# Weaving the two token blocks of the activations that are only stationary

## Chip, core and metric

One core of a Trainium2 chip runs the kernel. The metric is the device time of one execution in microseconds, the median of several runs. TensorE is called PE here, VectorE DVE, ScalarE ACT, GpSimd POOL, and SyncE SP.

## What is computed

256 tokens of width 1024 go through two blocks of two layers each; everything is float32. Cut to what matters here:

```
# block 1, two layers
proj = rms_norm(x, g_mix[l]) @ w_in[l]                 # 1024 x 10052
... four branches y_a, y_b, y_c, y_d, each ending in a @ w_o*[l] (512 x 1024)
merged = sum over branches of sigmoid(gate + b_gate) * y
x = x + merged @ w_merge[l]                             # 1024 x 1024
h2 = rms_norm(x, g_ffn[l])
gt = causal_dwconv(h2 @ w_ffn_gate[l], ffn_conv_w[l])   # 1024 x 2816
x = x + (silu(gt) * (h2 @ w_ffn_up[l])) @ w_ffn_down[l] # 2816 x 1024

# block 2, two layers
proj = rmsnorm(x, norm_w[l]) @ w_in[l]
y = concatenate([y_mla, y_gdn, y_moba])                 # 256 x 1024
x = x + y @ w_out[l]                                    # 1024 x 1024
```

## The kernel before

Weights stream from HBM into a ring of three slots of one megabyte (issued by SP, L2703). Each slot is cut into two parts, counted by `j`. For every part ACT writes a rounded high half, `whi` (L1173, `split_hi`, type fp32r), and DVE the remainder, `wlo` (L1755, `split_lo`); four parts are in flight, and both engines run four parts ahead of PE. The activations have the same two halves: `hhi` and `hlo` (8 channel chunks of 128 partitions x 256 tokens), `F[q] = (fhi, flo)` (4 chunks each) and, in block 2, `W0` and `W3` (2 chunks each, one tensor `fin`). A product is three passes in fp32r: high x high, low activation x high weight, high activation x low weight.

There are two ways to multiply a part:

- `chans` (from L484): the weights are the stationary operand (128 x 128) and the activation moves, 256 tokens. Output: channels by tokens. L499 holds the passes with `whi`, L508 that with `wlo`. A part has 24 matmuls of 256 columns.
- `toks` (from L512): 128 tokens of the activation are the stationary operand and 512 (in two places 324 and 416) weight columns move. Output: tokens by channels. L521 has the passes with `whi`, L529 that with `wlo`. A part of 512 columns has 12 matmuls: two token blocks `u`, two channel chunks `k`, three passes. `last_pair` (from L533, lines L544 and L551) does the last two parts of an accumulation, token block by token block.

`toks` and `last_pair` read the stationary operand as `s_[:, k0 + k, cols(u)]`: 128 tokens that lie side by side, 4 bytes apart; `cols(u)` is `slice(u * 128, u * 128 + 128)`.

Where `toks` and `last_pair` are used: some input projections of block 1 (`idx`, `aq`, `ak`, `av`, `sv`) and `m0` of block 2, all on the normed `hhi`/`hlo`, which `chans` also reads as the moving operand; the merge (merged activations, again written into `hhi`/`hlo` after the last use of the normed ones); FFN-down (`F`, the gated activations); and w_out of block 2 (`W0` and `W3` for chunks 0 and 3, `hhi`/`hlo` for 1 and 2, in the order 0, 3, 1, 2 of `OUT_ORDER`).

Who writes these: ACT copies the f32 values (`mer1`, `fy`, `yT`) into the high tensor (L1440 and L1449 for the merge, L1480 for the FFN, L1630 for block 2), and DVE subtracts that from the f32 values into the low one (L2175, L2255, L2545). All work on 2 chunks x 256 tokens. PE waits for the low one before the first part that needs it. The program of every engine is written out in order; side tasks (convolution, attention, delta rule) are interleaved with the parts at fixed places (`MIX_AT`, `TWO_AT`). Other matmuls go through two helpers, L469 (`group`) and L474 (`turn`, transposes), in plain f32.

## Time and profile before

| | |
|---|---|
| median of 3 runs | 1377.38 us (1377.34 to 1378.05) |
| span of the profiled execution | 1369.2 us |
| PE busy | 1345.0 us (98%), 10828 matmuls |
| DVE busy | 1040.0 us (76%) |
| ACT busy | 750.9 us (55%) |
| HBM read | 221.01 MB, mean 162 GB/s |

The span goes from the first to the last instruction of one profiled execution; of that execution the profile gives no other time. Engine rows give busy time, share of the span and instruction counts. A matmul is pipelined: its recorded duration overlaps the next one's, so what it costs a stream is the distance from its start to the next start. PEld is the load of the stationary operand, which goes on under the matmul before. In a group, the text `out<-moving,stationary` is followed by the rows and columns of the array that are in use and the number of partitions and elements of the moving operand; for PEld these are the stationary operand's. A row of busy times by stretch holds start:end, its length, then the busy time of PE, PEld, DVE, ACT and POOL with their counts, the granted clock, the share of the DMA engines and GB/s.

### The profile page before, as it was taken

To read this page: it belongs to the slowest core of one execution; us is meant where nothing else is said; L and a number is where in the kernel's file an instruction comes from. 1 tells how busy PE (TensorE), PEld (TensorE's weight loads), DVE (VectorE), ACT (ScalarE), POOL (GpSimd) and SP (SyncE) were. 2 spreads that over 40 slices of the span, in tenths; PEclk is the share of its full clock that TensorE was granted. 3 is DMA by queue.
4 is the path that set the end of the run, shared out by engine and by line. 5 is a ranking of instruction groups with operands and counts; after the bars stand their busy time and mean duration, and the time that the engine had idled before them with its cause. 6 is when DMAs were issued, how large, how long until landed. Compare 5 with 4: busy or idle time off the path is not lost. (4 is left out here: it accounts for less than half of the span.)

```text
span 1369.2 us, 26498 instructions
## 1 busy us (share of the span) xinstructions
PE 1345.0 (98%) x10828; PEld 1265.4 (92%) x10828; DVE 1040.0 (76%) x1781; ACT 750.9 (55%) x1157; POOL 46.3 (3%) x48
## 2 busy tenths in 40 slices
PE   8999999999999999999999999999999999999998
PEld 8899999998999989899999999999989899888996
DVE  6999898677766666999897767766778746777565
ACT  6544656556444455544557545544558546576363
POOL 0000000000000000000000000000000110001100
PEclk9999999999999999999999999999999999999999
DMA  8565444564665465645364555555553324353231
GB/s 289 177 207 178 131 154 160 180 215 155 197 202 185 139 230 163 215 155 185 97 204 159 187 187 172 198 185 191 178 186 124 120 64 137 100 174 109 78 102 69
DMA packets 108992, 223.77 MB, mean 163 GB/s; under 512 B 6180, under 2 KB 17700, under 8 KB 108872
## 3 DMA queue, kind: packets, MB, share of 16 engines
q1 hardware_dynamic: 106736, 219.12, 48.2%
q10 hardware_dynamic: 2136, 2.96, 0.7%
q8 instruction: 86, 1.41, 0.4%
q14 instruction: 34, 0.28, 0.1%
HBM read 221.01 MB, written 1.06 MB: 162 GB/s over the span
## 5 line engine op out<-in xcount | busy, mean ns | idle before, releaser
L1755 DVE TENSOR_TENSOR wlo<-ring,whi 128x1024 fp32r<-128x1024 f32 (+3 forms) x430 | 498.1, 1180 | 182.7 <-ACT whi L1173 152.7
L1173 ACT ACTIVATE whi<-ring 128x1024 fp32r<-128x1024 f32 (+3 forms) x430 | 433.2, 1026 | 361.8 <-PE bank L499 228.7
L499 PE MATMUL bank<-hhi,whi 128*128 128x256 f32 x2016 | 278.8, 280 | 6.0 <-ACT sgb L1431 3.9
L508 PE MATMUL bank<-hhi,wlo 128*128 128x256 f32 x2016 | 280.3, 281 | 0.0
L499 PE MATMUL bank<-hlo,whi 128*128 128x256 f32 x2016 | 275.3, 278 | 0.0
L499 PEld LDWEIGHTS bank<-hhi,whi 128*128 128x128 f32 x2016 | 253.1, 189 | 9.5 <-ACT sgb L1431 4.3
L508 PEld LDWEIGHTS bank<-hhi,wlo 128*128 128x128 f32 x2016 | 252.6, 189 | 3.7 <-issue 2.6
L499 PEld LDWEIGHTS bank<-hlo,whi 128*128 128x128 f32 x2016 | 251.6, 189 | 0.0
L469 PE MATMUL bank<-w 64*64 64x64 f32 (+5 forms) x1376 | 101.7, 249 | 1.5 <-DMA w<-in_flip 0.9
L1935 DVE SCALAR_TENSOR_TENSOR w<-w,par 128x256 f32<-128x256 f32 x240 | 98.0, 478 | 0.0
L521 PE MATMUL bank<-whi,hhi 128*128 128x512 f32 (+2 forms) x256 | 96.6, 379 | 0.0
L521 PE MATMUL bank<-whi,hlo 128*128 128x512 f32 (+2 forms) x256 | 96.1, 377 | 0.0
L469 PEld LDWEIGHTS bank<-w 64*64 64x64 f32 (+3 forms) x1376 | 84.1, 150 | 10.7 <-issue 2.6
L2615 POOL TENSOR_TENSOR st<-st,mhalf 128x1 f32<-128x1 f32 (+2 forms) x34 | 33.3, 979 | 1224.9 <-DVE st L1776 558.0
L529 PE MATMUL bank<-wlo,hhi 128*128 128x512 f32 (+2 forms) x256 | 65.2, 377 | 0.0
L521 PE MATMUL bank<-whi,flo 128*128 128x512 f32 x160 | 62.6, 392 | 0.0
L521 PE MATMUL bank<-whi,fhi 128*128 128x512 f32 x160 | 62.5, 391 | 0.0
L521 PEld LDWEIGHTS bank<-whi,hhi 128*128 128x128 f32 x256 | 48.1, 188 | 8.9 <-issue 0.9
L521 PEld LDWEIGHTS bank<-whi,hlo 128*128 128x128 f32 x256 | 48.1, 188 | 7.6
L529 PEld LDWEIGHTS bank<-wlo,hhi 128*128 128x128 f32 x256 | 47.0, 188 | 8.0
L529 PE MATMUL bank<-wlo,fhi 128*128 128x512 f32 x160 | 43.2, 392 | 0.0
L2238 DVE SCALAR_TENSOR_TENSOR w<-w,par 128x256 f32<-128x256 f32 x88 | 36.7, 478 | 0.0
(309 smaller groups left out, 1535.5 us busy)
## 6 DMA issues: line engine op xcount, KB each, us to landing
ring<-in_w_in SPq DMA_DIRECT2D x100, 1024.0 KB, 5.1
ring<-in_w_ffn_down SPq DMA_DIRECT2D x22, 1024.0 KB, 5.1
ring<-in_w_ffn_gate SPq DMA_DIRECT2D x20, 1024.0 KB, 5.1
ring<-in_w_ffn_up SPq DMA_DIRECT2D x20, 1024.0 KB, 5.1
ring<-in_w_merge SPq DMA_DIRECT2D x8, 1024.0 KB, 5.1
ring<-in_w_out SPq DMA_DIRECT2D x8, 1024.0 KB, 5.0
ring<-in_w_oc SPq DMA_DIRECT2D x4, 1024.0 KB, 5.3
ring<-in_w_od SPq DMA_DIRECT2D x4, 1024.0 KB, 5.2
```

Of the source, the lines that this page charges most:

```text
L469: done = e.matmul(o, l_, r_, start=start and i == 0, stop=stop and i == len(pairs) - 1)
L499: done = e.matmul(o, wh[:, k, cols(u)], s_[:, k0 + k, :], stop=False, skip_group_check=True, start=opens and k == 0 and s_ is sh and u % 2 ...
L508: done = e.matmul(o, wl[:, k, cols(u)], sh[:, k0 + k, :], start=False, stop=closes, skip_group_check=True)
L521: done = e.matmul(held[u][:, 0:n], s_[:, k0 + k, cols(u)], wh[:, k, 0:n], stop=False, start=opens and k == 0 and s_ is sh, skip_group_chec ...
L529: done = e.matmul(held[u][:, 0:n], sh[:, k0 + k, cols(u)], wl[:, k, 0:n], start=False, stop=closes, skip_group_check=True)
L1173: e.activation(part_of(whi, j), part_raw(j), ACT.Copy).then_inc(*up("hi.a"))
L1755: e.tensor_tensor(part_of(wlo, j), part_raw(j), part_of(whi, j), ALU.subtract).then_inc(*up("lo.v"))
L1935: e.scalar_tensor_tensor(out=cacc[:, c], in0=glup[:, c, j:j + S], scalar=wv, in1=cacc[:, c], op0=ALU.mult, op1=ALU.add).then_inc(*up(name))
L2238: e.scalar_tensor_tensor(out=y, in0=g, scalar=wv, in1=y, op0=ALU.mult, op1=ALU.add).then_inc(*up("ffn.v"))
L2615: e.tensor_tensor(dst, src, half(n), ALU.pow).then_inc(*up(name))
```

## The change

Two views are added. `woven_toks` reads a tensor's 256 token places as 128 pairs: token `t * 128 + i` lies at place `2 * i + t`, so the tokens of one block are 8 bytes apart, with the other block's between them. `plain_toks` gives the same four dimensions on a contiguous tensor. The writers of the merged, gated and block-2 activations (ACT's copy and DVE's subtraction) write through `woven_toks`, and the merge, FFN-down and w_out read their stationary operands through it. The input projections read through `plain_toks`, which gives the same addresses as before. No instruction is added or removed, and no wait or queue changes.

```diff
--- before.py
+++ after.py
@@ -248,6 +248,12 @@
 
         def cols(h):
             return slice(h * P, h * P + P)
+
+        def woven_toks(ap):
+            return ap.rearrange("p c (i t) -> p c t i", t=2)
+
+        def plain_toks(ap):
+            return ap.rearrange("p c (t i) -> p c t i", t=2)
 
 
         A1, B1, vAf = part1(0, 1024), part1(1024, 1024), part1(2048, 1024)
@@ -509,16 +515,16 @@
                                         skip_group_check=True)
                 done.then_inc(*up("second.p"))
 
-            def toks(j, held, n, src, k0, opens, closes, mid=None):
+            def toks(j, held, n, src, k0, opens, closes, mid=None, weave=False):
 
                 wh, wl = part_of(whi, j), part_of(wlo, j)
-                sh, sl = src
+                sh, sl = (woven_toks(s_) if weave else plain_toks(s_) for s_ in src)
                 kn = wh.shape[1]
                 e.wait_ge(SEM["hi.a"], j + 1)
                 for u in range(2):
                     for k in range(kn):
                         for s_ in (sh, sl):
-                            done = e.matmul(held[u][:, 0:n], s_[:, k0 + k, cols(u)], wh[:, k, 0:n], stop=False,
+                            done = e.matmul(held[u][:, 0:n], s_[:, k0 + k, u], wh[:, k, 0:n], stop=False,
                                             start=opens and k == 0 and s_ is sh, skip_group_check=True)
                 done.then_inc(*up("first.p"))
                 if mid:
@@ -526,14 +532,14 @@
                 low_ready(j)
                 for u in range(2):
                     for k in range(kn):
-                        done = e.matmul(held[u][:, 0:n], sh[:, k0 + k, cols(u)], wl[:, k, 0:n], start=False, stop=closes,
+                        done = e.matmul(held[u][:, 0:n], sh[:, k0 + k, u], wl[:, k, 0:n], start=False, stop=closes,
                                         skip_group_check=True)
                 done.then_inc(*up("second.p"))
 
             def last_pair(j, acc, src, k0, tag, l):
 
 
-                sh, sl = src
+                sh, sl = (woven_toks(s_) for s_ in src)
                 for tb in range(2):
                     for nh in range(2):
                         wh, wl = part_of(whi, j + nh), part_of(wlo, j + nh)
@@ -541,14 +547,14 @@
                             e.wait_ge(SEM["hi.a"], j + nh + 1)
                         for k in range(2):
                             for s_ in (sh, sl):
-                                done = e.matmul(acc[nh][tb][:, :], s_[:, k0 + k, cols(tb)], wh[:, k, :], start=False,
+                                done = e.matmul(acc[nh][tb][:, :], s_[:, k0 + k, tb], wh[:, k, :], start=False,
                                                 stop=False, skip_group_check=True)
                         if tb == 0:
                             low_ready(j + nh)
                         else:
                             done.then_inc(*up("first.p"))
                         for k in range(2):
-                            done = e.matmul(acc[nh][tb][:, :], sh[:, k0 + k, cols(tb)], wl[:, k, :], start=False, stop=True,
+                            done = e.matmul(acc[nh][tb][:, :], sh[:, k0 + k, tb], wl[:, k, :], start=False, stop=True,
                                             skip_group_check=True)
                         if tb == 0:
                             done.then_inc(*up("norm.p"))
@@ -766,7 +772,7 @@
                 for c in range(3):
                     e.wait_ge(*at("mlo", l, c))
                     for nh in range(2):
-                        toks(j, [acc[nh], acc[2 + nh]], 512, hh, 2 * c, c == 0, False)
+                        toks(j, [acc[nh], acc[2 + nh]], 512, hh, 2 * c, c == 0, False, weave=True)
                         j += 1
                 e.wait_ge(*at("mlo", l, 3))
                 last_pair(j, [[acc[nh], acc[2 + nh]] for nh in range(2)], hh, 6, "mix", l)
@@ -779,7 +785,7 @@
                     for k in range(0, n, 2):
                         e.wait_ge(*at("f", l, i6, k // 2))
                         for nh in range(2):
-                            toks(j, [acc[nh], acc[2 + nh]], 512, F[i6 % 2], k, i6 == 0 and k == 0, False)
+                            toks(j, [acc[nh], acc[2 + nh]], 512, F[i6 % 2], k, i6 == 0 and k == 0, False, weave=True)
                             j += 1
                             put("second.p", "down", l, i6, nh)
                     return j
@@ -1124,7 +1130,7 @@
                     for nh in range(2):
                         if n == 0:
                             acc[nh] = [ps.take(e, "m", "wout", l, 2 * tb + nh) for tb in range(2)]
-                        toks(j, acc[nh], 512, src, k0, n == 0, False, between(j))
+                        toks(j, acc[nh], 512, src, k0, n == 0, False, between(j), weave=True)
                         behind(j)
                         j += 1
 
@@ -1437,7 +1443,8 @@
                                 if q == 0:
                                     e.wait_ge(*at(name, "gate", l, hf))
                                 e.wait_ge(*at("merged", l, 3, q))
-                                e.activation(hhi[:, 2 * q:2 * q + 2], mer1[:, 2 * q:2 * q + 2], ACT.Copy).then_inc(*up("mix.a"))
+                                e.activation(woven_toks(hhi[:, 2 * q:2 * q + 2]), plain_toks(mer1[:, 2 * q:2 * q + 2]),
+                                             ACT.Copy).then_inc(*up("mix.a"))
                                 put("mix.a", "mhi", l, q)
                         for i in range(2):
                             side.run(MIX_AT.get(2 * (j - mix0(l)), ()))
@@ -1446,7 +1453,8 @@
                             j += 1
                 for q in range(2, 4):
                     e.wait_ge(*at("merged", l, 3, q))
-                    e.activation(hhi[:, 2 * q:2 * q + 2], mer1[:, 2 * q:2 * q + 2], ACT.Copy).then_inc(*up("mix.a"))
+                    e.activation(woven_toks(hhi[:, 2 * q:2 * q + 2]), plain_toks(mer1[:, 2 * q:2 * q + 2]),
+                                 ACT.Copy).then_inc(*up("mix.a"))
                     put("mix.a", "mhi", l, q)
                 for i in range(6):
                     split_to(j + 4)
@@ -1477,7 +1485,8 @@
                         e.wait_ge(*at("fy", l, i6, i))
                         if i6 > 1:
                             e.wait_ge(*at("down", l, i6 - 2, 1))
-                        e.activation(F[i6 % 2][0][:, 2 * i:2 * i + 2], fy[:, 2 * i:2 * i + 2], ACT.Copy).then_inc(*up("ffn.a"))
+                        e.activation(woven_toks(F[i6 % 2][0][:, 2 * i:2 * i + 2]), plain_toks(fy[:, 2 * i:2 * i + 2]),
+                                     ACT.Copy).then_inc(*up("ffn.a"))
                         put("ffn.a", "f", "hi", l, i6, i)
                     for i in range(4 if i6 else 0):
                         split_to(j + 4)
@@ -1627,7 +1636,7 @@
                         e.wait_ge(*at("mla" if c == 0 else "moba", "gated", l))
                         e.wait_ge(*at("mla", "lg", l, 1, 1))
                         dst = (W0 if c == 0 else W3)[0]
-                    e.activation(dst, yT[:, 2 * c:2 * c + 2], ACT.Copy).then_inc(*up("outs.a"))
+                    e.activation(woven_toks(dst), plain_toks(yT[:, 2 * c:2 * c + 2]), ACT.Copy).then_inc(*up("outs.a"))
                     put("outs.a", "fin", "hi", l, c)
 
 
@@ -2172,8 +2181,8 @@
 
                 def low_v(q):
                     e.wait_ge(*at("mhi", l, q))
-                    e.tensor_tensor(hlo[:, 2 * q:2 * q + 2], mer1[:, 2 * q:2 * q + 2], hhi[:, 2 * q:2 * q + 2],
-                                    ALU.subtract).then_inc(*up("mix.v"))
+                    e.tensor_tensor(woven_toks(hlo[:, 2 * q:2 * q + 2]), plain_toks(mer1[:, 2 * q:2 * q + 2]),
+                                    woven_toks(hhi[:, 2 * q:2 * q + 2]), ALU.subtract).then_inc(*up("mix.v"))
                     put("mix.v", "mlo", l, q)
 
                 for n_b, (key, bi, name, _) in enumerate(BRANCHES):
@@ -2252,7 +2261,8 @@
                         leave("ffn.v", "up", l, i6, i)
                         put("ffn.v", "fy", l, i6, i)
                         e.wait_ge(*at("f", "hi", l, i6, i))
-                        e.tensor_tensor(F[i6 % 2][1][:, 2 * i:2 * i + 2], y2, F[i6 % 2][0][:, 2 * i:2 * i + 2],
+                        e.tensor_tensor(woven_toks(F[i6 % 2][1][:, 2 * i:2 * i + 2]), plain_toks(y2),
+                                        woven_toks(F[i6 % 2][0][:, 2 * i:2 * i + 2]),
                                         ALU.subtract).then_inc(*up("ffn.v"))
                         put("ffn.v", "f", l, i6, i)
                     for i in range(4 if i6 else 0):
@@ -2542,7 +2552,7 @@
                         e.tensor_tensor(y2, y2, g, ALU.mult).then_inc(*up("outs.v"))
                         put("outs.v", tag, "gated", l)
                     e.wait_ge(*at("fin", "hi", l, c))
-                    e.tensor_tensor(lo, y2, hi, ALU.subtract).then_inc(*up("outs.v"))
+                    e.tensor_tensor(woven_toks(lo), plain_toks(y2), woven_toks(hi), ALU.subtract).then_inc(*up("outs.v"))
                     put("outs.v", "fin", l, c)
 
 
```

## Rows read from the trace of the kernel before

**Rows 1.** The page: span, busy times, granted clock and GB/s in 40 slices.

```profile
span 1369.2 us, 26498 instructions
...
PE 1345.0 (98%) x10828; PEld 1265.4 (92%) x10828; DVE 1040.0 (76%) x1781; ACT 750.9 (55%) x1157; POOL 46.3 (3%) x48
...
PEclk9999999999999999999999999999999999999999
...
GB/s 289 177 207 178 131 154 160 180 215 155 197 202 185 139 230 163 215 155 185 97 204 159 187 187 172 198 185 191 178 186 124 120 64 137 100 174 109 78 102 69
```

**Rows 2.** The waits of PE: total, times, longest; the largest.

```profile
PE bank L499 <- ACT sgb L1431: 3.9, 2, 2.0
```

**Rows 3.** Groups by form of PE: count | busy us, mean ns | idle before.

```profile
L521 PE MATMUL bank<-whi,hhi 128*128 128x512 f32 x192 | 75.5, 393 | 0.0
...
L521 PE MATMUL bank<-whi,fhi 128*128 128x512 f32 x160 | 62.5, 391 | 0.0
...
L521 PE MATMUL bank<-whi,fin 128*128 128x512 f32 x64 | 16.1, 394 | 0.0
...
L544 PE MATMUL bank<-whi,hhi 128*128 128x512 f32 x32 | 12.5, 391 | 0.0
...
L544 PE MATMUL bank<-whi,fhi 128*128 128x512 f32 x16 | 6.3, 391 | 0.0
```

**Rows 4.** Timeline of PE, merge and FFN-down: start us, us, instruction.

```profile
301.91 0.39 PE L521 MATMUL bank<-whi,hhi 128*128 128x512 f32 x1
...
304.66 0.39 PE L521 MATMUL bank<-whi,hhi 128*128 128x512 f32 x1
...
318.39 0.39 PE L544 MATMUL bank<-whi,hhi 128*128 128x512 f32 x1
...
371.96 0.39 PE L521 MATMUL bank<-whi,fhi 128*128 128x512 f32 x1
372.19 0.39 PE L521 MATMUL bank<-whi,flo 128*128 128x512 f32 x1
```

**Rows 5.** Timeline: plain f32 matmuls of 256 columns; loads under one-column matmuls.

```profile
226.52 1.89 PE L469 MATMUL bank<-xn 128*128 128x256 f32 x8
...
1334.84 1.87 PEld L469 LDWEIGHTS bank<-onesb,w 128*128 128x128 f32 x16
```

**Rows 6.** Timeline of PE: 324 columns, 512 in another rhythm, 256.

```profile
36.77 0.31 PE L521 MATMUL bank<-whi,hhi 128*128 128x324 f32 x1
...
38.55 0.31 PE L521 MATMUL bank<-whi,hhi 128*128 128x324 f32 x1
...
98.34 0.40 PE L521 MATMUL bank<-whi,hhi 128*128 128x512 f32 x1
...
101.15 0.40 PE L521 MATMUL bank<-whi,hhi 128*128 128x512 f32 x1
...
298.29 1.07 PE L508 MATMUL bank<-fhi,wlo 128*128 128x256 f32 x8
```

**Rows 7.** Writers (by form; by line: count, min/median/max, first and last start); a stretch's busy times.

```profile
L1480 ACT ACTIVATE fhi<-w 128x512 fp32r<-128x512 f32 x22 | 13.9, 632 | 41.0 <-DVE w L2251 41.0
...
L2255 DVE TENSOR_TENSOR flo<-w,fhi x22: 691/693/694, 354.4 to 997.1; 128x512 fp32r<-128x512 f32 x22
...
L2175 DVE TENSOR_TENSOR hlo<-w,hhi x4: 684/692/694, 298.8 to 308.3; 128x512 fp32r<-128x512 f32 x4
...
372.00:383.00 11.00, 11.00 (x51) 9.03 (x50) 8.53 (x9) 6.15 (x8) 0.00 (x0) 1.00 0.50 165
```

**Rows 8.** Timeline of w_out in the last layer, all engines.

```profile
1348.86 1.99 PE L521 MATMUL bank<-whi,fin 128*128 128x512 f32 x8
...
1350.42 1.29 DVE L2545 TENSOR_TENSOR hlo<-w,hhi 128x512 fp32r<-128x512 f32 x2
...
1351.38 0.19 PEld L521 LDWEIGHTS bank<-whi,hhi 128*128 128x128 f32 x1
```

## Prediction

> **What bounds the kernel now.** I read the page first, its shares and its 40 slices. TensorE (PE) is busy 98% of a span of 1369.2 us, in nearly every slice, at a granted clock of 9 tenths or more in all of them, the level of 2.4 GHz; VectorE (DVE) is busy 76% and ScalarE (ACT) 55% [rows 1]. Then the waits of PE: the largest adds up to 3.9 us, and none stands on the lines that the change touches, L521, L529, L544 and L551 (the row kept is the largest) [rows 2]. So what PE does between the starts of two matmuls sets the time, and a nanosecond there is worth its count. The median of the runs is 1377.38 us, 8.2 us above the profiled span (what lies around the span and between runs); I make the sum against the span and carry it over to the median unchanged.
>
> The groups by form give the counts. The woven matmuls are those with an activation as the stationary operand (128x128) and 512 weight columns moving: L521 fhi 160 + flo 160, L529 fhi 160, L544 fhi 16 + flo 16, L551 fhi 16, that is 528 for FFN-down; L521 fin 64 (high and low) and half as many on L529, that is 96; L544 hhi 32 + hlo 32 and L551 hhi 32, that is 96 (of each name one row stands; its low twin and its second pass have the same count) [rows 3]. Of the three groups of 192 on hhi and hlo at L521 and L529, a third each is woven: by the loops, merge has 2 layers x 3 chunks x 2 halves of N x 4 matmuls = 48 and w_out's third chunk 2 x 2 x 4 = 16, so 64 a group, 192 together [rows 3]. In all 528 + 96 + 96 + 192 = 912. The other 3 x 128 = 384 with 512 columns belong to the block-1 input projections, where hhi is also a moving operand elsewhere; they keep the contiguous layout.
>
> The number to look at is not a matmul's recorded duration (391 ns, pipelined) but the distance between starts. In the merge the parts of 12 matmuls start at 301.91, 304.66 and so on, and the 72nd matmul after the first starts at 318.39: 16.48 us / 72 = 228.9 ns [rows 4]. FFN-down starts its second matmul 0.23 us after the first, and the eight of w_out take 1.99 us, (1.99 - 0.39) / 7 = 229 ns [rows 4, 8]. There is no idle time in those rows. I use 229.0 ns. At 2.4 GHz 512 columns are 213.3 ns, so 15.7 ns of each are not columns.
>
> **What the 15.7 ns may be.** Each matmul has a load of 128 columns under it. The load is not the bound: with one moving column 16 loads take 1.87 us, (1.87 - 0.19) / 15 = 112 ns apiece [rows 5], half of 229. Plain f32 matmuls with 256 columns take 1.89 us for eight, (1.89 - 0.379) / 7 = 215.9 ns: they spend two array cycles a column, so the same 213.3 ns of array time and the same load of 128 columns, with 2.6 ns on top [rows 5]. What differs is that their moving operand is read half as fast. So 13.1 ns appear only where the moving operand is read at 4 bytes per array cycle. Two more observations. The excess is mostly not proportional to the columns: with 324 columns a part of twelve takes 38.55 - 36.77 = 1.78 us, 148.3 ns each, of which 135.0 are columns, 13.3 ns of excess against 15.7 [rows 6]. And the same instructions on the same tiles come in another rhythm elsewhere: 101.15 - 98.34 = 2.81 us for twelve, 234 ns each [rows 6]. An excess that changes while shapes, tiles and clock stay is an interference that depends on how two streams fall against each other, and the two streams of PE are the load and the moving operand. With 256 columns (32 matmuls from 298.29 to 301.91, 113.1 ns) the load's 112 ns binds and says little [rows 6].
>
> **The change, part by part.** (1) The step of the load. Before, the load walks 128 x 4 = 512 bytes in 112 ns, 4.6 bytes/ns, while the moving operand walks 2048 bytes in 213.3 ns, 9.6 bytes/ns: one overtakes the other, and they can meet again and again. Woven, the load walks 1024 bytes in 112 ns, 9.1 bytes/ns, nearly abreast of the moving operand. After a first meeting both keep their distance. No row shows a load with this step, so the price is bounded: it may take away all 13.1 ns, down to the nearest row without interference, 215.9 ns (the bare columns would be 213.3, 15.7 ns less), or nothing, or it may add as much again, 13.1 ns, if what costs is the address range that the load touches, which doubles. I take the full removal, because the f32 row has the same array time and load and sits at 215.9, and the rates match: 912 x 13.1 ns = 11.9 us less. The bounds are -14.3 us and +11.9 us.
>
> The page "TensorE: Matmul & The Clock Gate" of the Trainium skill (section on what happens when you issue a matmul) says that the load and the streaming operand have independent SBUF read ports and that the load takes nothing from a running matmul. The rows above have 13.1 ns that this rule doesn't explain; by the rule the sum would be 0 and the time stay. The page "SBUF — State Buffer" (Specifications) states cachelines of 16 bytes that want at least two hits each: a step of 8 bytes just has its two, so no slower load, but 64 lines instead of 32. If each line opened costs the moving operand something, that rule speaks against the change.
>
> (2) The writers. 22 ACT copies of 632 ns for FFN, and by the loops 8 for the merge and 8 for w_out, write with the step now, 38 in all, and as many DVE subtractions of about 692 ns [rows 7]. Whether the step slows them no row shows. Between 0 and twice as long, that is 0 to 24 us of ACT and 0 to 26 us of DVE over engines idle 45% and 24% of the span [rows 1]; below nothing is excluded, since the element count is the same. I take 0. The cover: FFN's first low part starts at 354.4 and is first used at 371.96, 17 us later; the merge's first starts at 298.8 for a matmul at 301.91, and its last at 308.3 for those at 318.39 [rows 4, 7]. Doubling them reaches none of these. Queued behind them on ACT and DVE are the weight splits of the next parts. In a stretch of FFN-down DVE is busy 8.53 of 11.00 us and ACT 6.15 [rows 7]; with PE through in 10.4 us DVE stands at 82%, and with each of its subtractions twice as long (two in a chunk of 33 us) hardly higher.
>
> (3) What is late next. In w_out chunk 1 waits for its low part: the pair of subtractions starts at 1350.42, of the two, 1.29 us together, the first ends near 1351.1, and the load that needs it is at 1351.38, 0.27 us of slack [rows 8]. The four parts before it (48 matmuls) shrink by 0.6 us. The subtraction is queued behind a weight split on DVE, and that behind ACT's, which partly follow PE; so the new wait is 0 to 0.36 us per layer. I take 0.1 us per layer, 0.2 together. If the writers were twice as long, 0.7 us per layer would come on top at this one place. DMA: in the same stretch its engines are busy half the time at 165 GB/s, and 6% more is far under the 289 GB/s of the first slice [rows 1, 7].
>
> Sum: 1377.4 - 11.9 + 0.2 = 1365.7 us.
>
> **Rivals.**
> A. Half of it. The meeting remains in part, or the load itself takes longer because each 16 of its elements now spread over twice the bytes: at twice 112 ns the load would bind at 224 ns, 5 ns less than now, 912 x 5 = 4.6 us; half the interference gone is 6.0 us. Time about 1371 to 1373. For it: two streams of 9.1 and 9.6 bytes/ns still drift by some 60 bytes in a load.
> B. Nothing. The 15.7 ns belong to a moving operand read at full rate, whatever the load does; the step changes nothing and the writers are hidden. 1377.4 us, 0.2 us up at most. The independent ports of the skill's page on TensorE would make it this case. For it: 324 and 512 columns can be read as a line with 0.429 ns a column and 9.2 ns fixed, and nothing in it must be a collision. Against: the second rhythm of 234 ns.
> C. Slower. Each load touches twice the range, and each new piece of it stops the moving operand: 13.1 ns become 26.2, the start distance 242, 912 x 13.1 = 11.9 us more, 1389.3 us. It shows as slower once the distance is over 229.0 + 2.75 us / 912 = 232 ns. For it: 234 ns exist already in this trace, so worse meetings are possible; and abreast can also mean always in the same place. Against: 2.4 GHz columns stalled once lag by that much for good, and a stalled stream leaves the place.
>
> **How the numbers follow.** Full removal 0.52 (0.03 of it down to the bare columns, 1363.1), A 0.16, B 0.17, C 0.15. The predicted time is that of the full removal, 1365.7 us. The range holds full removal, A and B: from 1362.5 (bare columns, less the spread of runs) to 1378.0 (B with the small wait and the spread); C's 0.15 is left out. 0.2% of 1377 is 2.75 us, about what a measurement of this kernel can tell from no change; full removal and A are beyond it: faster 0.68, same 0.17, slower 0.15.
>
> **What would show it.** Right: the starts on L521, L529, L544 and L551 with fhi, flo and fin 216 ns apart, a merge part every 2.59 us, while the 384 contiguous ones of the input projections stay at 229 and 234 and the 256-column ones at 113. The two-sided price: a distance near 224 points to a slower load, one above 232 to rival C. Writers: the rows of L1480 and L2255 at 632 and 692 ns. Wrong would be the whole argument if the contiguous ones moved with them, or if PE's waits gained a row on hhi, hlo, fhi or flo of over 1 us.

## Result and the profile after

The changed kernel takes 1383.47 us (median, 1382.14 to 1384.55); the kernel before, on the same chip, 1377.36 us (1373.62 to 1378.05). The ratio is 1.0048, with a 95% interval of 1.0031 to 1.0066: slower by 0.5%, where 11.7 us less was forecast, and outside the range of 1362.5 to 1378.0.

The page of after, with the lines that answer [rows 1]:

```profile
span 1382.8 us, 26498 instructions
...
PE 1359.0 (98%) x10828; PEld 1281.9 (93%) x10828; DVE 1040.4 (75%) x1781; ACT 752.0 (54%) x1157; POOL 46.2 (3%) x48
...
PEclk9999999999999999999999999999999999999999
```

The instruction count is the same, PE is again busy 98%, at 9 tenths or more in every slice. The span is 13.6 us longer, and PE is busy 14.0 us more, at the same number of matmuls. The waits of PE show nothing new; the largest is the one of [rows 2], unchanged:

```profile
PE bank L505 <- ACT sgb L1437: 3.9, 2, 2.0
```

So matmuls became slower, and the timeline of PE in the first FFN-down of after says which (start us, us, instruction; line L527 is L521 of before, L505 is L499, L514 is L508; matmuls of flo and of L535 between are left out, x8 stands for eight in a row):

```profile
303.75 0.40 PE L527 MATMUL bank<-whi,hhi 128*128 128x512 f32 x1
...
306.56 0.39 PE L527 MATMUL bank<-whi,hhi 128*128 128x512 f32 x1
...
374.21 0.40 PE L527 MATMUL bank<-whi,fhi 128*128 128x512 f32 x1
...
377.02 0.39 PE L527 MATMUL bank<-whi,fhi 128*128 128x512 f32 x1
...
385.42 1.10 PE L505 MATMUL bank<-hhi,whi 128*128 128x256 f32 x8
386.36 1.10 PE L505 MATMUL bank<-hlo,whi 128*128 128x256 f32 x8
387.30 1.10 PE L514 MATMUL bank<-hhi,wlo 128*128 128x256 f32 x8
...
391.07 1.11 PE L505 MATMUL bank<-hhi,whi 128*128 128x256 f32 x8
```

A woven part of twelve takes 2.81 us, in the merge as in FFN-down, where it took 2.75 in [rows 4]. Four parts, 48 matmuls, take 385.42 - 374.21 = 11.21 us, 233.5 ns each against 229.0. And there is a second thing, which the change does not touch in the code at all: the matmuls of 256 columns behind it, the gate weights of the FFN, take 391.07 - 385.42 = 5.65 us for 48, 117.7 ns each. The same place in the timeline of before:

```profile
382.95 1.09 PE L499 MATMUL bank<-hhi,whi 128*128 128x256 f32 x8
383.88 1.07 PE L499 MATMUL bank<-hlo,whi 128*128 128x256 f32 x8
384.79 1.07 PE L508 MATMUL bank<-hhi,wlo 128*128 128x256 f32 x8
```

There eight of them take 384.79 - 383.88 = 0.91 us, 113.4 ns each (the next ones as well; only the first eight take 0.93). I call 113.4 ns the fast rhythm of the narrow matmuls (256 columns) and 117.7 the slow one. Both occur in both kernels, with PE never idle in them: a stretch keeps its rhythm over hundreds of matmuls, and it changes only where other matmuls or a wait come between. Behind FFN-down it is fast in all eight stretches of before (in each of two layers three of 192 matmuls and one of 96) and slow in all eight of after.

The bill for the 13.6 us between the two spans:

- 912 woven matmuls x 4.4 ns = 4.0 us.
- 1344 narrow matmuls behind FFN-down x 4.3 ns = 5.8 us. As a test of both terms together: a layer's FFN-down with what stands behind it holds 264 woven and 672 narrow ones, 1.16 + 2.89 = 4.05 us; counted off matmul by matmul the difference grows by 4.02 us over it in either layer.
- 1.6 us near 1225 us, where the granted clock of after falls to half for some 3 us and that of before does not:

```profile
1225.00:1226.00 1.00, 1.00 (x9) 1.00 (x8) 1.00 (x4) 0.92 (x4) 0.00 (x0) 0.64 0.16 59
1226.00:1227.00 1.00, 1.00 (x6) 1.00 (x6) 1.00 (x3) 0.99 (x2) 0.00 (x0) 0.50 0.01 4
```

  (Busy times of PE, PEld, DVE, ACT and POOL by stretch, then the granted clock, 1.00 for 2.4 GHz and 0.50 for 1.2.) A wait for DVE stands just before it in both kernels, 1.22 us in after and 1.24 in before. Of the ten traces of the whole kernel shown or named below, the clock falls here in five (after, e3_writers, e5_settled, e7_before_settled and e11_rest_only), with and without woven reads, and in five not (before, e4, e2, e6, e10); after and e10 are the same kernel. So it is chance and not the weave. Two more such falls, near 170 and 670 us, stand in both traces and so not in the bill.
- 0.9 us in the first 12 us (a wait for the first input: the first narrow matmul starts at 12.94 us instead of 12.00) and 0.8 us in the first 192 narrow matmuls, which are in the slow rhythm here and in the fast one in before; both lie ahead of the first woven instruction.

That is 13.1 of 13.6 us; the rest is small differences of both signs. The first two entries, 9.8 us, go with the weave, the other 3.3 us don't. The medians are only 6.1 us apart: the timed runs of before took some 6 us more than its traced one, and on what is not known, since none of them was traced. In the other comparisons below the kernel before has medians of 1370.95, 1371.11 and 1375.51 us.

What of the prediction's other rows answers: the contiguous matmuls did not move (the 144 of the input projections from 43.88 us on start 229.0 ns apart in both traces). The writers, by form (busy us, mean ns, idle before), to be held against [rows 7], and the load of the woven operand:

```profile
L527 PEld LDWEIGHTS bank<-whi,fhi 128*128 128x128 f32 x160 | 31.3, 196 | 6.0
...
L2264 DVE TENSOR_TENSOR flo<-w,fhi 128x512 fp32r<-128x512 f32 x22 | 15.3, 696 | 16.2 <-ACT fhi L1488 16.2
...
L1488 ACT ACTIVATE fhi<-w 128x512 fp32r<-128x512 f32 x22 | 14.7, 668 | 40.7 <-DVE w L2260 40.7
```

ACT's copy is 36 ns longer (632 in before), DVE's subtraction 3 (693). The load's record says 196 ns; before it said 188:

```profile
L521 PEld LDWEIGHTS bank<-whi,fhi 128*128 128x128 f32 x160 | 30.0, 188 | 6.2
```

In w_out the third term's wait did not come, since the woven parts did not shrink: chunk 1's low part is written from 1363.76 us on (a pair of 1.29 us, the first done near 1364.45), and its load starts at 1364.78, with 0.33 us to spare.

### The profile page after: what moved, and what is told of

Read it like the earlier page. It is cut to its first block and busy times, and to the rows that moved or that the text cites. A ratio compares the mean times of both kernels' runs of the same rounds, so it can differ in the third digit from the quotient of the medians.

```text
span 1382.8 us, 26498 instructions
## 1 busy us (share of the span) xinstructions
PE 1359.0 (98%) x10828; PEld 1281.9 (93%) x10828; DVE 1040.4 (75%) x1781; ACT 752.0 (54%) x1157; POOL 46.2 (3%) x48
## 5 line engine op out<-in xcount | busy, mean ns | idle before, releaser
L505 PE MATMUL bank<-hhi,whi 128*128 128x256 f32 x2016 | 280.9, 281 | 6.2 <-ACT sgb L1437 3.9
L514 PE MATMUL bank<-hhi,wlo 128*128 128x256 f32 x2016 | 283.3, 282 | 0.0
L505 PE MATMUL bank<-hlo,whi 128*128 128x256 f32 x2016 | 278.1, 280 | 0.0
L505 PEld LDWEIGHTS bank<-hhi,whi 128*128 128x128 f32 x2016 | 255.0, 189 | 9.6 <-ACT sgb L1437 4.3
L514 PEld LDWEIGHTS bank<-hhi,wlo 128*128 128x128 f32 x2016 | 255.4, 190 | 3.7 <-issue 2.6
L505 PEld LDWEIGHTS bank<-hlo,whi 128*128 128x128 f32 x2016 | 254.0, 189 | 0.0
L1944 DVE SCALAR_TENSOR_TENSOR w<-w,par 128x256 f32<-128x256 f32 x240 | 98.1, 478 | 0.0
L527 PE MATMUL bank<-whi,hhi 128*128 128x512 f32 (+2 forms) x256 | 97.0, 380 | 0.0
L527 PE MATMUL bank<-whi,hlo 128*128 128x512 f32 (+2 forms) x256 | 96.4, 378 | 0.0
L535 PE MATMUL bank<-wlo,hhi 128*128 128x512 f32 (+2 forms) x256 | 65.5, 378 | 0.0
L527 PE MATMUL bank<-whi,fhi 128*128 128x512 f32 x160 | 63.4, 396 | 0.0
L527 PE MATMUL bank<-whi,flo 128*128 128x512 f32 x160 | 63.2, 395 | 0.0
L527 PEld LDWEIGHTS bank<-whi,hhi 128*128 128x128 f32 x256 | 48.6, 190 | 8.8 <-issue 0.9
L527 PEld LDWEIGHTS bank<-whi,hlo 128*128 128x128 f32 x256 | 48.5, 190 | 7.3
L535 PEld LDWEIGHTS bank<-wlo,hhi 128*128 128x128 f32 x256 | 47.4, 190 | 7.8
L535 PE MATMUL bank<-wlo,fhi 128*128 128x512 f32 x160 | 43.8, 395 | 0.0
L527 PEld LDWEIGHTS bank<-whi,fhi 128*128 128x128 f32 x160 | 31.3, 196 | 6.0
```

The source lines that it names most:

```text
L505: done = e.matmul(o, wh[:, k, cols(u)], s_[:, k0 + k, :], stop=False, skip_group_check=True, start=opens and k == 0 and s_ is sh and u % 2 ...
L514: done = e.matmul(o, wl[:, k, cols(u)], sh[:, k0 + k, :], start=False, stop=closes, skip_group_check=True)
L527: done = e.matmul(held[u][:, 0:n], s_[:, k0 + k, u], wh[:, k, 0:n], stop=False, start=opens and k == 0 and s_ is sh, skip_group_check=True)
L535: done = e.matmul(held[u][:, 0:n], sh[:, k0 + k, u], wl[:, k, 0:n], start=False, stop=closes, skip_group_check=True)
L1944: e.scalar_tensor_tensor(out=cacc[:, c], in0=glup[:, c, j:j + S], scalar=wv, in1=cacc[:, c], op0=ALU.mult, op1=ALU.add).then_inc(*up(name))
```

## Experiments

Theory 1, after this reading: the load of an 8-byte step is itself longer, this costs the woven matmuls 4.4 ns each, and the rhythm in which PE leaves them is handed on to the narrow ones behind (this last part did not hold as a rule, see under e3_writers). Its rivals: the writers do it; what follows is chance of one run; the narrow ones are slow for a reason of their own.

**e1_micro: the step by itself.** A small kernel without the computation, in which only the step of the stationary operand differs:

```
for s in (1, 2, 3, 4, 8):            # step in elements of 4 bytes
    stationary = g[s][:, c].rearrange("p (i t) -> p t i", t=s)[:, u]
    # 12, 24 ... matmuls of 512 columns, between narrow ones of 256
```

> A kernel of its own that leaves out the whole computation and only streams matmuls: 24-matmul blocks of 256 columns with weights as the stationary operand, three times twelve matmuls of 512 columns whose stationary operand has a step of 4, 8, 12, 16 or 32 bytes, then 256 columns again; each stretch after a short pause; then loads under 64 moving columns, and plain f32 matmuls of 256 columns, by step. Theory 1 (the step disturbs the stream): 229 ns between starts at 4 bytes, 233 to 234 at 8 bytes as in the changed kernel, more at 16 and 32, since fewer elements share a neighbourhood; the load under 64 columns stays at 112 ns at 4 and 8 bytes. Theory 2 (only the rhythm that a stretch happens to start with): 229 or 234 at every step, mixed between the two passes over the steps. Theory 3 (inherited rhythm): the 256-column matmuls after a stretch of 4 bytes settle at 113.4 ns, those after 8 bytes at 117.7, whatever the ones before had.

Timeline of PE, first the step of 4 bytes, then of 8 (x8 of high and low, L221 between them left out):

```profile
256.66 1.98 PE L217 MATMUL bank<-whi,g 128*128 128x512 f32 x8
...
267.54 1.98 PE L217 MATMUL bank<-whi,g 128*128 128x512 f32 x8
...
273.57 2.03 PE L217 MATMUL bank<-whi,g 128*128 128x512 f32 x8
...
284.77 2.03 PE L217 MATMUL bank<-whi,g 128*128 128x512 f32 x8
```

48 matmuls take 10.88 us at 4 bytes, 226.7 ns each, and 11.20 us at 8 bytes, 233.3 ns. Over all passes it was 227 at 4 bytes, 233.0 at 8, 235 at 12 and at 16, 244.6 at 32. So the step costs some 6 ns here with no ACT, DVE or DMA at work: it is a matter of PE and its reads alone. But the narrow matmuls ran at about 120 ns after every step; the handing on (Theory 3) did not show in this kernel. The loads under 64 columns missed too: at a granted clock of 1.00 they took 112 ns at 4 bytes, but 117 to 118 at 8, where 112 was expected. Plain f32 matmuls of 256 columns had 215.8 ns at both steps.

**e2_readers and e3_writers: halves of the change.** In the first only the reads of the stationary operands are woven, and the writers store contiguously:

```diff
-e.activation(woven_toks(F[i6 % 2][0][:, 2 * i:2 * i + 2]), plain_toks(fy[:, 2 * i:2 * i + 2]), ACT.Copy)
+e.activation(plain_toks(F[i6 % 2][0][:, 2 * i:2 * i + 2]), plain_toks(fy[:, 2 * i:2 * i + 2]), ACT.Copy)
```

and so for the other writers; in the second it is the reverse:

```diff
-                sh, sl = (woven_toks(s_) if weave else plain_toks(s_) for s_ in src)
+                sh, sl = (plain_toks(s_) for s_ in src)
```

> Only the readers weave: merge, FFN-down and w_out load their stationary operand with 8 bytes from tensors written contiguously, so the tokens come out in another order; everything else as before. Theory 1 (the loads do it): all of the loss, ratio 1.004 to 1.005 to the kernel before, 233.3 ns on the 912 matmuls and 117.7 ns on the 256-column ones behind FFN-down. Rival (the writers do it): ratio 1.000, 229 ns.

> Only the writers weave, the readers load 128 neighbouring places, which now hold tokens of both blocks (order changed, amount of work the same). Theory 1 (the loads do it): ratio 1.000, 229 ns, 632 ns a copy on ScalarE and 692 ns a subtraction on VectorE as before. Rival (the step of the writes costs, or delays a split behind it): ratio 1.004, and longer copies or PE waits.

Reads alone: 1382.89 us, ratio 1.0084 (1.0067 to 1.0101). Writers alone: 1372.1 us, ratio 1.0008 (0.9999 to 1.0018). The reads carry the loss; the writers' 36 and 3 ns are covered, as the prediction said. Two numbers expected were missed: the ratio of the reads, 1.004 to 1.005, and the copy of e3_writers, 632 ns, which took 667 (632 in e2_readers). The load's record is 195 ns in e2_readers and 188 in e3_writers. The first FFN-down in the timeline of e3_writers, where the reads are contiguous:

```profile
374.96 0.40 PE L527 MATMUL bank<-whi,fhi 128*128 128x512 f32 x1
...
386.16 1.09 PE L505 MATMUL bank<-hhi,whi 128*128 128x256 f32 x8
387.09 1.07 PE L505 MATMUL bank<-hlo,whi 128*128 128x256 f32 x8
387.99 1.07 PE L514 MATMUL bank<-hhi,wlo 128*128 128x256 f32 x8
```

This one stretch is a surprise: contiguous, and yet 11.20 us for 48, 233.3 ns. In this run the 384 narrow matmuls ahead of it were in the slow rhythm; the seven other FFN-down stretches, entered from fast narrow ones, have 228.9. So a contiguous stretch can be slow too, when it is entered in the slow rhythm. (The first FFN-down of e11_rest_only is a second case. The 24 contiguous ones of [rows 6], from 98.34 us on, bear it out as well: they have 228.8 ns in the three cases of twenty in which the narrow ones ahead are fast, and 233.4 to 233.5 in the seventeen in which those are slow.) But the stretch of e3_writers leaves the fast rhythm behind: 0.90 to 0.91 us for eight. In e2_readers the same happens once in each layer (entered slow, left fast); the other six of its eight narrow stretches are slow. The handing on is therefore a strong tendency of the woven loads and not a law.

Nor is it the stretch's own distance that is handed on. In the timeline of before, the 144 contiguous matmuls of the input projections, 229.0 ns apart, leave slow narrow ones behind them without any pause:

```profile
75.07 1.10 PE L499 MATMUL bank<-hhi,whi 128*128 128x256 f32 x8
76.02 1.11 PE L499 MATMUL bank<-hlo,whi 128*128 128x256 f32 x8
```

0.95 us for eight. It is so in both layers of all nine traces in which nothing is inserted there, 18 of 18. A contiguous stretch can thus leave either rhythm, and what decides between this place and FFN-down no run shows. What the runs do show is that at FFN-down the weave turns what stands behind from fast to slow.

**e4_before_again: how much a run of before differs from another.** The kernel before, unchanged.

> The kernel before, once more. Its first profile has a span of 1369.2 us, while three of four timed runs are at 1377 us; the changed kernel's profile lies within 2 us of its timed runs. Theory (the 256-column streams take one of two rhythms, 113.4 or 117.7 ns, partly by chance of where they start): this profile has about 6 us more than the first, all of it in 256-column streams at 117.7 that were at 113.4. Rival (the time lies outside the matmul streams): the streams show the same rhythms as the first profile.

1369.6 us, span 1367.8. This missed: I had looked for the several microseconds between the profiled run and the median of before, and this run is again a short one, its span 1.4 us below the first. Its rhythms aren't quite those of the first trace: the 144 narrow matmuls from 81.5 us on (`sq`, `sk`) are fast here and slow there (-0.7 us with what is behind them). Larger is a difference that is no rhythm: in the first trace the granted clock falls to half for 3.4 us near 168 us, and here it does not (-1.6 us); a wait of 0.94 us at 193.58 us, which the first does not have, and slow narrow matmuls give the 1.5 us back.

```profile
168.00:169.00 1.00, 1.00 (x7) 1.00 (x6) 1.00 (x2) 0.14 (x1) 0.00 (x0) 0.50 0.00 0
```

(The first trace.) Rhythms, falls of the clock and the first wait thus all vary from run to run. The kernel before takes 1369 to 1378 us in its runs; which of the three makes the longer ones long is not shown, as none of them was traced. Behind FFN-down all eight are fast again.

**e5_settled: undo the handing on, keep the weave.** Two plain f32 matmuls of one column between each woven FFN-down and the narrow ones:

```diff
+            def settle(o, n=2):
+                for _ in range(n):
+                    e.matmul(o[:, 0:1], onesb[:, :], onesb[:, 0:1], start=True, stop=True)
@@ chans
+                if opens and j in [ffn0(l_) + 20 + 12 * q_ for l_ in range(L) for q_ in range(4)]:
+                    settle(held[0])
```

> The changed kernel with two one-column f32 matmuls before the first matmul of each gate group that follows an FFN-down (4 places a layer, 16 matmuls of about 112 ns, 1.8 us in all). In five traces a stretch of 256-column matmuls behind one-column matmuls ran at 113.4 ns every time (10 of 10), behind the woven FFN-down at 117.7 in 13 of 17. Theory (the woven stretch hands its slower rhythm on, and that is more than half of the loss): these stretches go to 113.4, 1344 x 4.3 ns = 5.8 us less, with the cost 4 us less than the changed kernel, about 1379 us; the woven matmuls stay at 233.3. Rival (the slower 256-column matmuls have their own cause): 117.7 stays, the time is 2 us over the changed kernel's.

```profile
371.59 0.40 PE L534 MATMUL bank<-whi,fhi 128*128 128x512 f32 x1
...
382.79 0.50 PE L493 MATMUL bank<-onesb 128*128 128x1 f32 x4
383.15 1.16 PE L512 MATMUL bank<-hhi,whi 128*128 128x256 f32 x8
384.15 1.07 PE L512 MATMUL bank<-hlo,whi 128*128 128x256 f32 x8
385.06 1.07 PE L521 MATMUL bank<-hhi,wlo 128*128 128x256 f32 x8
```

(Each f32 matmul of one column has two records, so x4 is the two.) The woven stretch takes 382.79 - 371.59 = 11.20 us for 48, as in after, while the narrow ones behind are fast again, 385.06 - 384.15 = 0.91 us for eight, in all eight places. Both claims hold: the 4.4 ns belong to the woven loads, and the 4.3 ns of the narrow ones are no cost of the narrow ones' own. The insertion itself costs 0.36 us until the next narrow start and 0.09 more in the first eight, 0.45 us each, 3.6 in all, so a gain of 5.8 - 3.6 = 2.2 us over the changed kernel should be left, where 4 were expected. The median is 1379.2 us, ratio 1.0063 (1.0046 to 1.008) against a before of 1370.95 in that comparison. The changed kernel did not run in it, so the gain itself isn't measured. It is no way back to the time of before.

**e6_down_only and e11_rest_only: the change in two pieces.** Only FFN-down and its writers woven (528 matmuls), and only the merge and w_out (384):

```diff
 # e6_down_only
-                sh, sl = (woven_toks(s_) for s_ in src)
+                sh, sl = ((woven_toks if tag == "ffn" else plain_toks)(s_) for s_ in src)
 # e11_rest_only
-                sh, sl = (woven_toks(s_) for s_ in src)
+                sh, sl = ((plain_toks if tag == "ffn" else woven_toks)(s_) for s_ in src)
```

with `weave=True` and the writers of the other piece taken back as well.

> Only FFN-down is woven; merge and w_out are written and read as before. Theory (own cost 4.4 ns on 528 matmuls, 2.3 us, plus the inherited rhythm on up to 1344 narrow matmuls, 5.8 us): about 8 us of the change's loss of 10 to 12 stays, ratio 1.005 to 1.007. Rival (only the matmuls' own cost, in proportion to their number 528 of 912): ratio 1.002 to 1.003.

> Only merge and w_out are woven (384 of the 912 matmuls), FFN-down as before. Behind merge and w_out come norms with pauses, so there is no narrow stretch to inherit. Theory (own cost plus inheritance): 384 x 4.4 ns = 1.7 us, ratio 1.001 to 1.002, and the stretches behind FFN-down at 113.4. Rival (the loss has another source, common to all woven parts): in proportion 384 / 912 of the whole, 1.0035.

FFN-down alone: 1379.96 us, ratio 1.0067 (1.0052 to 1.0082); that is 9.2 us (7.1 to 11.2) where the two terms give 528 x 4.4 ns + 5.8 us = 8.1 us. The rest alone: 1376.71 us, ratio 1.0006 (0.9995 to 1.0018), 0.8 us (-0.7 to 2.5) where 384 x 4.4 ns give 1.7. Both hold within their intervals. Two timelines, of e6_down_only behind its second woven stretch:

```profile
416.85 1.10 PE L505 MATMUL bank<-hhi,whi 128*128 128x256 f32 x8
417.79 1.11 PE L505 MATMUL bank<-hlo,whi 128*128 128x256 f32 x8
418.74 1.10 PE L514 MATMUL bank<-hhi,wlo 128*128 128x256 f32 x8
```

and of e11_rest_only, the same stretch, contiguous, and what is behind it:

```profile
407.25 0.39 PE L527 MATMUL bank<-whi,fhi 128*128 128x512 f32 x1
...
418.23 1.10 PE L505 MATMUL bank<-hhi,whi 128*128 128x256 f32 x8
419.17 1.07 PE L505 MATMUL bank<-hlo,whi 128*128 128x256 f32 x8
420.07 1.07 PE L514 MATMUL bank<-hhi,wlo 128*128 128x256 f32 x8
```

0.94 to 0.95 us for eight against 0.90, and 10.98 us for the 48 of 512 columns, 228.8 ns.

**e7_before_settled: the same insertion in the kernel before**, ahead of its slow narrow stretches:

```diff
@@ chans (before)
+                if opens and j in [j_ for l_ in range(L) for j_ in (mix0(l_), mix0(l_) + 24, mix0(l_) + 28, mix0(l_) + 44, ffn0(l_))]:
+                    settle(held[0])
```

> The kernel before with the same two one-column matmuls before five groups of a layer whose narrow matmuls often run at 117.7 ns (glu_b, sq, sk, gb and the FFN's first gate): 20 extra matmuls, 2.2 us. If they settle the rhythm, up to 5 x 96 x 2 narrow matmuls gain 4.3 ns, 4.1 us, and the time falls by about 2 us with less spread; if not, it rises by 2 us.

1377.66 us, ratio 1.0055 (1.004 to 1.007): missed. Behind seven of the ten insertions the narrow matmuls are fast, behind three they are slow. Two of the three even stand between 48 narrow matmuls at 113.4 ns and 96 at 117.7 ns; this is the timeline of the first:

```profile
88.13 0.50 PE L487 MATMUL bank<-onesb 128*128 128x1 f32 x4
...
89.52 1.10 PE L506 MATMUL bank<-hlo,whi 128*128 128x256 f32 x8
90.46 1.11 PE L515 MATMUL bank<-hhi,wlo 128*128 128x256 f32 x8
```

(0.94 us for eight behind it, 0.91 ahead.) So the insertion does not set the fast rhythm everywhere, as it did in the eight places of e5_settled. In each layer 48, 48 of 144 and 160 of 240 slow narrow matmuls became fast, 2.2 us in both layers, and each of the ten insertions costs 0.45 us as above, 4.5 us. That is 2.3 us more. By the last FFN-down of block 1 this trace is 3.1 us behind the one of before (995.72 against 992.66 us), of which 1.0 us lies in the first wait, ahead of the first narrow matmul, and 2.0 are left for the insertions. Of the 6.5 us between the two spans the rest lies in block 2, which has no insertion: 0.8 us up to 1190 us, 1.0 in waits behind that, and the fall of the clock for 1.6. The rhythm of the narrow matmuls can be bent by hand, but not at a profit in this way, and the price of the insertion was set too low: 2.2 us for the twenty extra matmuls, where they cost 4.5.

**e8_micro2: an attempt to bring the fast rhythm about outside the kernel**, with the tensors at the places that they have in the kernel, and narrow stretches behind 512-column ones at both steps, one-column ones and plain f32 ones:

```
[narrow 24] [512 columns x24, step 4 or 8 bytes] [narrow 48]
[narrow 24] [f32, 1, 128, 256 or 512 columns]     [narrow 48]
```

> A kernel of its own without the computation: the tensors lie as in the real kernel; after a pause one part of 24 narrow matmuls, then something else, then two parts narrow; the something is 2 or 4 parts of 512 columns at 4 or at 8 bytes, one, two or four f32 matmuls of one column, f32 ones of 128, 256 or 512 columns; three times each. Theory (the rhythm is a relation in time between load and moving operand that the last matmuls leave behind): 512 columns at 4 bytes run at 229 and leave 113.4 behind; at 8 bytes they run at 233.3 and leave 117.7 more often than not; the one-column ones leave 113.4. Rival (chance): both rhythms behind each of them, in no relation.

```profile
32.10 0.39 PE L216 MATMUL bank<-whi,hhi 128*128 128x512 f32 x1
...
37.69 1.10 PE L229 MATMUL bank<-hhi,whi 128*128 128x256 f32 x8
...
46.65 0.39 PE L216 MATMUL bank<-whi,hhi 128*128 128x512 f32 x1
...
52.25 1.11 PE L229 MATMUL bank<-hhi,whi 128*128 128x256 f32 x8
```

At 4 bytes 5.59 us for 24, 232.9 ns, at 8 bytes 5.60, 233.3. Narrow ones settled at 117 to 119 ns throughout, and nothing put ahead of them brought 113.4. So this kernel is in the slow rhythm all the time, and in it both steps cost the same. That agrees with the contiguous stretch of 233.3 in e3_writers and says nothing on how the fast rhythm comes about. Inconclusive for its purpose.

**e9_micro3: is the excess over the columns a matter of the load at all?** With 512 columns moving, the load is cut to 96, 64 and 32 columns; then the moving operand is cut with a full load; then loads under 64 columns at steps of 0 to 32 bytes:

```
mm(step=1, load=128 | 96 | 64 | 32, moving=512);  mm(step=0, load=128, moving=512);  mm(step=2, load=64, moving=512)
mm(step=1 | 2, load=128, moving=128 | 192 | 256 | 320 | 384 | 448 | 512)
mm(step=0 | 1 | 2 | 3 | 4 | 8, load=128, moving=64)
```

> A kernel of its own without the computation. (a) 36 matmuls of 512 columns whose stationary operand has 128, 96, 64 or 32 columns at 4 bytes, 128 columns with a step of 0, and 64 at 8 bytes. If the excess over 213.3 ns is an interference between the load and the moving operand, as the prediction had it, it falls with the columns loaded: 227 to 229 at 128, about 221 at 64, 216 at 32 and near 216 at step 0. If it belongs to the moving operand alone (rival B of the prediction), it stays at 227 to 229 for all. (b) The same with 128 to 512 moving columns at 4 and at 8 bytes: if a woven load simply takes longer, the two differ where the load binds (128 to 256 columns: 112 against 118 ns) and by 4 to 6 ns still at 512. (c) Twelve loads under 64 columns between plain f32 matmuls that keep the clock up: 112 ns at 4 bytes, 118 at 8, over 118 at 12 and 16, 233 or less at 32 bytes.

Timeline of PE; each row is one block, and its first distance (0.42 us at 512 columns, 0.22 at 64) is the change from plain f32. The array's rows and columns in use stand before the moving operand:

```profile
49.95 8.56 PE L222 MATMUL bank<-whi,g 128*128 128x512 f32 x36
...
69.21 8.63 PE L222 MATMUL bank<-whi,g 128*64 128x512 f32 x36
...
78.87 8.69 PE L222 MATMUL bank<-whi,g 128*32 128x512 f32 x36
...
221.41 1.61 PE L222 MATMUL bank<-whi,g 128*128 128x64 f32 x12
...
230.17 1.68 PE L222 MATMUL bank<-whi,g 128*128 128x64 f32 x12
...
239.00 2.29 PE L222 MATMUL bank<-whi,g 128*128 128x64 f32 x12
...
248.44 2.96 PE L222 MATMUL bank<-whi,g 128*128 128x64 f32 x12
```

First three rows: (8.56 - 0.39 - 0.42) / 34 = 228 ns with a full load; with 96 and 64 columns loaded it is 230, with 32 it is 232. A load a quarter as long takes nothing away from the excess over 213.3 ns. With step 0, where all 128 columns come from one address, it is 229. So, at a step of 4 bytes, the load under it isn't what the excess is made of. Last four rows, where the load binds, at 4, 8, 12 and 16 bytes: twelve matmuls are 0.07 us longer at 8 bytes than at 4, 6 ns for each of 11 distances. Distance by distance the load takes 111.6 ns at 4 bytes, 117.8 at 8, 173.9 at 12, 233.4 at 16 and 238.0 at 32. At 8 bytes 128 columns moving have 117.8 ns as well, 256 have 119.9 at both steps, 320 and 384 the same at both steps (146.6 and 173.6). The expected 112 against 118 ns came up to 192 columns (111.6 against 118.8), the equality at 256 was not expected. With 448 columns the woven load is the faster one, 203.5 against 206.7 ns; with 512 it is the slower one (4 bytes, then 8):

```profile
153.48 8.54 PE L222 MATMUL bank<-whi,g 128*128 128x512 f32 x36
...
208.97 8.82 PE L222 MATMUL bank<-whi,g 128*128 128x512 f32 x36
```

Counted distance by distance that is 227.0 against 235.5 ns, 8.5 more where 4 to 6 were expected, though a load of 118 ns ends long before the matmul. With 64 columns loaded at 8 bytes it is 231.1 ns, against 229.9 at 4: this surcharge, other than the excess, does shrink with the load. At 32 bytes the load took 238.0 ns where 233 or less was expected.

**e10_after_again: the changed kernel again.**

> The changed kernel once more, beside the others of this call: ratio 1.008 as in the readers' run, 1382 to 1384 us, with 117.7 ns behind most FFN-downs.

1383.72 us (1380.88 to 1383.93), within the 1382 to 1384 expected; the ratio of 1.008 was missed, it is 1.0052 (1.0032 to 1.0073), with before at 1375.51. All eight narrow stretches behind FFN-down are slow again. With this the count is: behind contiguous FFN-down stretches 40 of 40 narrow ones fast (before, e3, e4, e7, e11), behind woven ones 30 of 32 slow (after, e2, e6, e10), behind woven ones with the insertion 8 of 8 fast (e5). That is no chance of one run. (That is for FFN-down; the places of e7 and of the input projections are told above.) In e10 the first FFN-down of layer 1 is entered in the slow rhythm and left in it, where the first of either layer of e2 was entered in the slow one and left in the fast one, so what decides in those cases is open.

## Why the prediction was wrong

**What bounds it** was read rightly: PE's start distances set the time, no wait changed, and a few nanoseconds of each moved the kernel by what they are worth. The 8.2 us between span and median were put down to what lies around the span and between runs, and carried over unchanged. The profiled run of after took 1384.55 us at a span of 1382.8, so 1.8 us lie around it; the other 6.4 us say that the profiled run of before was a short one. What the longer runs had more of, slow rhythms, falls of the clock or a longer first wait, no trace of them shows. That was visible in no row of the one trace, but a difference of 0.6% between two numbers of one kernel was a sign that its runs are not alike.

**Term (1), the step of the load, is the step that failed.** It rested on the premise that the 13.1 ns over the f32 row [rows 5] arise between load and moving operand and go when the load keeps abreast. e9_micro3 shows, in its small kernel, that they stay when the load is a quarter as long (232 ns) or reads one address (229 ns), so there was nothing for another step to take away. Rival B's statement on this point was the true one, and the page "TensorE: Matmul & The Clock Gate" of the Trainium skill (what happens when you issue a matmul) had it in its independent ports: the trace of e9 agrees for loads at 4 bytes, 228 to 232 ns whatever their length. At 8 bytes it doesn't: 235.5 ns against 227.0 there, 233.4 against 229.0 in the kernel. There the measurement decides. What stood against B, the second rhythm of 234 ns [rows 6], was taken for two streams in collision; for that stretch it goes with how it is entered, 228.8 ns behind narrow matmuls at 113.4 ns and 233.5 behind narrow ones at 117.7. Why plain f32 matmuls of the same array time have 215.9 ns no run shows; that the slower reading makes the difference was assumed.

The part that did depend on the step went the other way: the load alone is 6 ns longer at 8 bytes. In the prediction this was half of rival A, with 224 ns for a load twice as long, below the 229 of then, and so free. The page "SBUF — State Buffer" of the Trainium skill (Specifications) has lines of 16 bytes that want two hits, and a step of 8 bytes was expected to be as good as one of 4 by it; the runs show 111.6 and 117.8 ns, so the measurement decides: nearly as good, and not quite. From 8 to 12 bytes, below two hits a line, the load goes to 173.9, as that rule leads one to expect.

A load of 118 ns under a matmul of 229 should not bind. That it costs 4.4 ns all the same is what rival C describes in its direction: each matmul 233.4 against its bound of 232 for slower. Its size was a third of the 13.1 ns, and 912 x 4.4 ns = 4.0 us instead of 11.9. How a load that ends in time makes the stream longer has been shown as a fact (e1_micro, e2_readers) and not explained.

**What no case had** is the larger part: 5.8 us in matmuls that the diff doesn't touch. The prediction itself says that narrow ones at 113.1 ns are bound by a load of 112 and "say little" [rows 6], and its list of what would show it wrong has them at 113 throughout. In the trace of before the same narrow form stands at 117.7 ns in other stretches, and whether a stretch's rhythm depends on what ran before it could have been asked there. A rival C priced with 4 ns for the woven ones and 4 ns for their 1344 followers would have given 1387 us at most and 1381 at the least; that is hindsight.

**Term (2), the writers at 0**, was right: 36 and 3 ns longer, and 1.0008 (0.9999 to 1.0018) for the ratio of the writers alone. **Term (3), 0.2 us**, did not appear, because its cause, a shorter w_out, did not. **The chances:** 0.15 for C was too little for a case that had a measured hint behind it, the 234 ns; it was left out of the range by choice.

## What to carry to other kernels

Where matmuls are issued back to back without idle time, price a change of the stationary operand's layout with its own small kernel before building on an argument about rates: here 8 bytes of step cost the load 6 ns of 112, and 12 or 16 bytes cost 62 and 122. Read start distances stretch by stretch, also of the matmuls behind the changed ones, since instructions that the diff doesn't touch can fall into a rhythm of 4% more. And where one profiled execution stands 0.5% away from the median, trace more than one run, and look for stretches that have two rhythms and for falls of the clock, before explaining anything of that size.

## What the runs showed that was not expected

- Narrow fp32r matmuls (256 columns, full load) run at 113.4 or at 117.7 ns, and 512-column ones at 229.0 or 233.3, for hundreds in a row at the same granted clock of 1.00. Between narrow ones a contiguous 512-column stretch has 229.0 when entered from the fast rhythm and 233.3 when entered from the slow one; a woven one has 233.4 either way. Behind FFN-down the narrow ones are fast in 40 of 40 contiguous cases and slow in 30 of 32 woven ones. Behind the contiguous stretch of the input projections, at 229.0 ns itself, they are slow in 18 of 18, so the step is not all that decides.
- Behind two f32 matmuls of one column the fast rhythm stands in 8 of 8 cases of e5 and in 7 of 10 of e7, at a price of 0.45 us a place. None of the three small kernels ever showed 113.4 ns (e1 and e9 have 120, e8 117 to 119), so what the fast rhythm needs is open; placing the tensors as in the kernel was not it.
- In e9 the load of a stationary operand has 111.6, 117.8, 173.9, 233.4 and 238.0 ns at steps of 4, 8, 12, 16 and 32 bytes.
- The excess of a 512-column fp32r matmul over its columns stays at 14 to 18 ns when a load at 4 bytes under it is cut to a quarter. What a step of 8 bytes adds does shrink with the load: 8.5 ns with 128 columns loaded, 1.2 with 64.
